# Adding up the squares of the inner norms on VectorE alone, taking their sums inside the third unit, and rotating the mixing projections over four banks

## The chip, the core and the metric

The program runs on one core of a Trainium2 chip. The core has a matrix engine (TensorE, PE in the profile), a vector engine (VectorE, DVE), an activation engine (ScalarE, ACT), a general engine (GpSimd, POOL) and a queue that issues DMA transfers (SP). The metric is the device time of one execution in microseconds (us); three executions of the kernel before took 1939.79 to 1940.9 us.

## The reference

Two transformer blocks work on the same 512 tokens of width 1024. Reduced to their order, they are:

```
h = h + 0.5 * swiglu(rmsnorm(h, ffn1_norm))            # norm "ffn1"
u = rmsnorm(h, mix_norm); projections u @ w_in          # norm "mix": three attentions, gates
h = h + sum(gates * branches) @ w_out
h = h + 0.5 * swiglu(rmsnorm(h, ffn2_norm))            # norm "ffn2"
z = rmsnorm_2(h, g_mix_2) @ w_in_2 + b_in_2             # norm "mix2": conv of 31 taps, pooling
h = h + y @ w_out_2
h = h + swiglu_2(rmsnorm_2(h, g_ffn_2))                 # norm "ffn3"
out = rmsnorm_2(h, g_final_2)                           # norm "final"
# rmsnorm(x, g) = x * rsqrt(mean(x*x) + eps) * g
```

## The kernel before, in words

Activations lie transposed: features on the 128 partitions, the 512 tokens along the row, so that a width of 1024 is eight chunks (`DK`). The weights are one stream of units of 128 x 1024 numbers; a unit projects the eight input chunks onto 128 outputs, or spreads one chunk over eight outputs. Every fp32 product is made of three matmuls on rounded numbers: high by high, weights low by high, high by input low (`products`, L458 to L460). One unit is 24 matmuls.

Four raw units and two split units fit in memory. For unit u, ScalarE writes the high part (`high`, L851), which needs unit u-2 to be done by TensorE (its slot in `weights_high` becomes free); GpSimd then writes the low part (`low_part`, L384), and TensorE waits for that (`low_done`) before its first matmul of u. `after(u)` on ScalarE stands for "cast unit u+2".

A norm's factor per token is not applied to the input but to the outputs of the projections. At such a norm the input is made chunk by chunk: VectorE updates the residual (L1199), ScalarE writes the high part of the chunk times the gain (L861) and its square (L862), VectorE the low part (L1163). Meanwhile TensorE runs `pair_start`: the first two units, interleaved, unit two three chunks behind unit one, each chunk as its low part comes. The squares of chunks 0 to 4 are added by GpSimd (L400, four additions), those of 5 to 7 and the total by VectorE (L1180, three additions). TensorE then sums over the partitions with narrow matmuls (`sums`, L511), ScalarE takes the root (L867), VectorE the inverse (L1170), TensorE spreads the result over the partitions (`spread_factor`, L519), and VectorE copies it out of the bank (`token_factor`, L1189). Only then can VectorE take the outputs of the first units (L1214 and on; L1247 in the mixing stage of the first block, L1508 in that of the second).

The order on every engine is the order in which the code is written; engines meet by semaphores. On ScalarE, in `gate_up`, the cast of a stage's fifth unit (`after(u0 + 2)`) stands behind the silu and the high part (L972) of the first hidden chunk, both of which need the factor. In the mixing stages (`stepped`, and the loop over `IN2_STEPS`), it stands behind the square, or the sigmoid, of the second projection. The mixing projections go round over three banks: unit j waits until the output of unit j-3 was taken. After a projection of the first mixing stage TensorE makes the head norms' sums (L583) and the transposes (L593) of the projection before. In the second mixing stage VectorE and GpSimd also add up the taps of a convolution (L1473 and L443), on inputs that ScalarE scales.

## Time and profile before

| | |
|---|---|
| median of three runs | 1940.22 us |
| the profiled execution, first to last instruction | 1940.7 us |
| TensorE busy | 1863.6 us (96%) |
| VectorE busy | 893.9 us (46%) |
| ScalarE busy | 660.9 us (34%) |
| GpSimd busy | 848.8 us (44%) |
| mean granted TensorE clock | 0.985 |

The profiled execution's span and the median of the unprofiled runs are half a microsecond apart. A row of the timeline gives the start, the duration, the engine, the line of the kernel and the operation with what it writes and reads; in brackets stands how long the engine had been idle before, and what ended that. Matmul rows overlap: what counts for TensorE is the distance between starts.

### The profile page before, as it was taken

The page shows a single profiled execution, that of the slowest core. Times are in us where ns is not written, and L with a number is a line of the kernel's source. Part 1 is how long each engine was busy: PE and PEld are TensorE (multiplying, and loading weights), DVE is VectorE, ACT ScalarE, POOL GpSimd, SP SyncE. Part 2 cuts the span into 40 slices and gives each one's busy share as a digit, 9 for nine tenths or more (in the row PEclk, how much of TensorE's full clock was granted, in tenths as well). Part 3 has the DMA queues.
Part 4 walks back from the last instruction along what each step waited for, and adds up shares of the span by engine and source line. Part 5 has one row for each costly group of instructions (what it writes and reads, how often), then busy time and mean ns, then how long its engine had stood idle before and what let it go on. Part 6 is the DMA issues. An engine that isn't in the chain of part 4 may idle for free.

```text
span 1940.7 us, 22811 instructions
## 1 busy us (share of the span) xinstructions
PE 1863.6 (96%) x8194; PEld 1456.3 (75%) x8194; DVE 893.9 (46%) x1254; ACT 660.9 (34%) x1003; POOL 848.8 (44%) x379
## 2 busy tenths in 40 slices
PE   7999999999999999999999999999967999999997
PEld 5888888778776566667878888888753778888886
DVE  4333330377776876446633333302799353333102
ACT  4332321353223444446333323211523343332212
POOL 4444444544444322323454444444664254444443
PEclk9999999999999999999999999999987999999998
DMA  4222222323332111111222222222210122222221
GB/s 170 97 97 97 97 98 94 118 81 104 112 99 83 60 55 39 36 42 55 101 84 98 97 97 97 97 95 95 87 55 33 58 84 97 97 97 97 98 97 54
DMA packets 48763, 167.38 MB, mean 86 GB/s; under 512 B 5816, under 2 KB 6328, under 8 KB 48576
## 3 DMA queue, kind: packets, MB, share of 16 engines
q1 hardware_dynamic: 45216, 160.27, 23.6%
q10 hardware_dynamic: 3488, 6.31, 1.0%
q8 instruction: 38, 0.62, 0.1%
q14 instruction: 21, 0.17, 0.0%
HBM read 161.82 MB, written 2.11 MB: 84 GB/s over the span
## 4 chain that ended last, share of the span: by engine, by line
PE 86%; DVE 10%; ACT 2%; issue 1%; DMA 1%; ACTq 0%; DVEq 0%; SPq 0%
PE bank L458 23%; PE bank L460 23%; PE bank L459 23%; PE bank L640 7%; PE bank L674 4%; DVE conv_out L1473 3%; PE bank L702 3%; DVE input_low L1163 1%; PE bank L687 1%; DVE head_root L1302 1%; PE bank L790 1%; DVE tile L1293 1%; PE bank L583 1%; DVE residual L1199 1%; DVE tile L1294 1%
## 5 line engine op out<-in xcount | busy, mean ns | idle before, releaser
L384 POOL TENSOR_TENSOR weights_low<-raw_weights,weights_high 128x1024 fp32r<-128x1024 f32 x296 | 732.1, 2473 | 1070.3 <-ACT weights_high L851 1070.1
L458 PE MATMUL bank<-input_high,weights_high 128*128 128x512 f32 x1488 | 594.3, 399 | 39.6 <-DVE input_low L1163 20.9
L851 ACT CAST weights_high<-raw_weights 128x1024 fp32r<-128x1024 f32 x296 | 311.2, 1051 | 923.7 <-PE bank L460 883.9
L459 PE MATMUL bank<-input_high,weights_low 128*128 128x512 f32 x1488 | 584.7, 393 | 0.0
L460 PE MATMUL bank<-input_low,weights_high 128*128 128x512 f32 x1488 | 584.3, 393 | 0.0
L458 PEld LDWEIGHTS bank<-input_high,weights_high 128*128 128x128 f32 x1488 | 282.7, 190 | 113.2 <-issue 32.5
L460 PEld LDWEIGHTS bank<-input_low,weights_high 128*128 128x128 f32 x1488 | 282.5, 190 | 60.4
L459 PEld LDWEIGHTS bank<-input_high,weights_low 128*128 128x128 f32 x1488 | 282.9, 190 | 59.7 <-issue 2.6
L458 PE MATMUL bank<-hidden_high,weights_high 128*128 (+1 forms) x528 | 205.4, 389 | 0.0
L459 PE MATMUL bank<-hidden_high,weights_low 128*128 (+1 forms) x528 | 205.4, 389 | 0.0
L460 PE MATMUL bank<-hidden_low,weights_high 128*128 (+1 forms) x528 | 205.4, 389 | 0.0
L1219 DVE TENSOR_TENSOR tile<-bank,token_factor 128x512 f32<-128x512 f32 x66 | 45.6, 691 | 305.2 <-PE bank L460 305.2
L1229 DVE TENSOR_TENSOR hidden_low<-tile,hidden_high 128x512 f32 x66 | 122.6, 1857 | 58.7 <-ACT hidden_high L972 58.7
L1199 DVE SCALAR_TENSOR_TENSOR residual<-bank,residual 128x512 f32<-128x512 f32 x40 | 27.1, 683 | 262.5 <-PE bank L460 262.5
L459 PEld LDWEIGHTS bank<-hidden_high,weights_low 128*128 128x128 f32 x528 | 99.1, 188 | 20.7
L458 PEld LDWEIGHTS bank<-hidden_high,weights_high 128*128 128x128 f32 x528 | 99.1, 188 | 20.5
L460 PEld LDWEIGHTS bank<-hidden_low,weights_high 128*128 128x128 f32 x528 | 99.1, 188 | 20.5
L640 PE MATMUL bank<-input_high,weights_high 128*128 128x512 f32 x192 | 83.2, 434 | 0.0
L1473 DVE SCALAR_TENSOR_TENSOR conv_out<-glu_padded,vectors,conv_out 128x512 f32<-128x512 f32 x67 | 80.5, 1202 | 2.1
L640 PE MATMUL bank<-input_low,weights_high 128*128 128x512 f32 x192 | 81.0, 422 | 0.0
L640 PE MATMUL bank<-input_high,weights_low 128*128 128x512 f32 x192 | 80.8, 421 | 0.0
L1214 DVE TENSOR_TENSOR tile<-bank,token_factor 128x512 f32<-128x512 f32 x66 | 45.6, 691 | 66.6 <-PE bank L460 65.7
(219 smaller groups left out, 1890.4 us busy)
## 6 DMA issues: line engine op xcount, KB each, us to landing
raw_weights<-weights SPq DMA_DIRECT2D x296, 512.0 KB, 3.3
tile<-tile ACTq DMA_DIRECT2D x36, 64.0 KB, 2.2
residual<-x_t SPq DMA_DIRECT2D x4, 512.0 KB, 8.5
tile<-forget_sums ACTq DMA_DIRECT2D x8, 256.0 KB, 3.2
out_t<-out_t SPq DMA_DIRECT2D x8, 256.0 KB, 2.1
mem_in<-mem_t ACTq DMA_DIRECT2D x1, 1024.0 KB, 6.0
causal_mask<-causal_mask SPq DMA_DIRECT2D x1, 256.0 KB, 7.7
positions_in<-positions SPq DMA_DIRECT2D x1, 256.0 KB, 9.4
```

The source lines that it names most:

```text
L384: pool.tensor_tensor(wl[:, u % SPL, :], raw[:, u % RAW, :], wh[:, u % SPL, :].bitcast(F32), ALU.subtract).then_inc(low_done, 1)
L458: pe.matmul(out, wh[:, u % SPL, w], rh, start=start, stop=False)
L459: pe.matmul(out, wl[:, u % SPL, w], rh, start=False, stop=False)
L460: return pe.matmul(out, wh[:, u % SPL, w], rl, start=False, stop=stop)
L640: mm = pe.matmul(bank[g % 2][:, :], (wl if part == 1 else wh)[:, u % SPL, w], (xl if part == 2 else xh)[:, k, :], start=(k == 0 and part = ...
L674: mm = pe.matmul(bank[3 + n % 2][:, 0:ext], left, right, start=True, stop=(kind != "fox"))
L702: mm = pe.matmul(heads_bank(chunk_id(n))[lo:hi, q * P:(q + 1) * P], val, probs_t[s % 2][:, b * P:(b + 1) * P], start=(b == 0), stop=(b == ...
L851: act.copy(wh[:, u % SPL, :], raw[:, u % RAW, :]).then_inc(high_done, 1)
L1199: dve.scalar_tensor_tensor(out=h[:, m, :], in0=bank[m][:, :], scalar=share, in1=h[:, m, :], op0=ALU.mult, op1=ALU.add).then_inc(sem("resid ...
L1214: dve.tensor_tensor(tiles[c][:, :], bank[2 * c][:, :], rstd[:, :], ALU.mult).then_inc(sem(f"{name}_gate"), 1)
L1229: dve.tensor_tensor(hl[:, f, :].rearrange("p a n -> p (a n)"), tiles[2 + c][:, :], hh[:, f, :].rearrange("p a n -> p (a n)").bitcast(F32), ...
L1473: ins = dve.scalar_tensor_tensor(out=conv[:, c, :], in0=src, scalar=w, in1=conv[:, c, :], op0=ALU.mult, op1=ALU.add)
```

## The change

GpSimd no longer adds squares at the norms ffn1, mix, ffn2, mix2 and ffn3; VectorE adds all seven behind its last low part. At the final norm the old division stays. `sums` moves from the end of `pair_start` into the middle of the third unit (between its chunks 3 and 4), and `spread_factor` from ahead of the third unit to behind it. On ScalarE the cast of the fourth unit moves ahead of the root. The mixing projections use four banks, so that unit j waits for the output of j-4. In the first mixing stage the sums and transposes of projections 0 and 1 move into the middle of the fourth unit.

```diff
-        proj = [bank[0], bank[1], bank[7]]
+        proj = [bank[0], bank[1], bank[7], bank[3]]
+        proj2 = [bank[0], bank[1], bank[7], bank[6]]
...
+        def totalled(name):
+
+            return (INPUTS.index(name) + 1) * (DK - 1) - (POOL_SQUARES - 1) * (name == "final")
...
             low_part(0)
             low_part(1)
-            add_squares("ffn1")
             low_parts(2, U_IN + 2)
-            add_squares("mix")
...
+            def project(u, out, rh, rl, low_at, n=S, halfway=None):
                 pe.wait_ge(low_done, low_at)
                 for k in range(DK):
+                    if halfway and k == DK // 2:
+                        halfway()
                     mm = products(out, u, k, rh[:, k, 0:n], rl[:, k, 0:n], k == 0, k == DK - 1)
...
-                pe.wait_ge(sem("squares_totalled"), (INPUTS.index(name) + 1) * (DK - POOL_SQUARES))
+                pe.wait_ge(sem("squares_totalled"), totalled(name))
...
                 pair_start(feed, u0, bank[0][:, :], bank[1][:, :])
+                project(u0 + 2, bank[2][:, :], xh, xl, u0 + 3, halfway=lambda: sums(feed))
                 spread_factor(feed)
-                project(u0 + 2, bank[2][:, :], xh, xl, u0 + 3)
                 project(u0 + 3, bank[3][:, :], xh, xl, u0 + 4)
...
+            def finish(i):
+
+                kind, n = IN_STEPS[i], tokens(IN_STEPS[i])
+                if kind in NORM:
+                    k = upto_step(IN_STEPS, NORM, i)
+
+                    pe.wait_ge(sem("in_squared"), k)
+                    if k > 1:
+                        pe.wait_ge(sem("in_rooted"), k - 1)
+                    pe.matmul(bank[2][:, 0:n], (bd if heads(kind) == 2 else ones)[:, :],
+                              sq_in[k % 2][:, 0:n], start=True, stop=True).then_inc(sem("in_summed"), 1)
...
-                        if j >= 3:
-
-                            pe.wait_ge(sem("in_taken"), j - 2)
+                        if j >= 4:
+
+                            pe.wait_ge(sem("in_taken"), j - 3)
                         if IN_STEPS[j] == "km" and chunk_of(IN_STEPS, j) == 0:
                             pe.wait_ge(sem("mem_low"), DK)
+                        rh, rl = (mem_h, mem_l) if n == MEM else (xh, xl)
+                        project(U_IN + j, proj[j % 4][:, 0:n], rh, rl, U_IN + j + 1, n,
+                                halfway={2: lambda: sums("mix"), 3: lambda: (finish(0), finish(1))}.get(j))
                         if j == 2:
                             spread_factor("mix")
...
+                    if 3 <= j <= n_steps:
+                        finish(j - 1)
...
-            pair_start("mix2", U_IN2, proj[0][:, :], proj[1][:, :])
+            pair_start("mix2", U_IN2, proj2[0][:, :], proj2[1][:, :])
             for j in range(2, len(IN2_STEPS)):
-                if j >= 3:
-
-                    pe.wait_ge(sem("in2_taken"), j - 2)
+                if j >= 4:
+
+                    pe.wait_ge(sem("in2_taken"), j - 3)
+                project(U_IN2 + j, proj2[j % 4][:, :], xh, xl, U_IN2 + j + 1,
+                        halfway=(lambda: sums("mix2")) if j == 2 else None)
                 if j == 2:
                     spread_factor("mix2")
...
-                        after(U_IN + j)
+                        if j != 1:
+                            after(U_IN + j)
                         if j == 0:
+                            after(U_IN + 1)
                             feed_root("mix", bank[4])
...
                         after(u0 + 2 * c, i)
                         if c == 0 and i is None:
+                            after(u0 + 1)
                             feed_root(feed_name, bank[4])
-                            after(u0 + 1)
...
-                after(U_IN2 + j)
+                if j != 1:
+                    after(U_IN2 + j)
                 if j == 0:
+                    after(U_IN2 + 1)
...
+                for m in range(1, DK):
+                    dve.wait_ge(sem("input_square"), fed(name, m))
+                    dve.tensor_tensor(tiles[0][:, :], tiles[0][:, :], tiles[m][:, :], ALU.add
+                                      ).then_inc(sem("squares_totalled"), 1)
+                    dve.wait_ge(sem("squares_totalled"), INPUTS.index(name) * (DK - 1) + m)
```

On TensorE, at the norm ahead of the second feed-forward network (ffn2), before: `L511` are the sums, `L519` the spread, and the row that waits for `low_done` opens the third unit.

```order
L460 MATMUL bank<-input_low,weights_high 128x512
L511 MATMUL bank<-ones,tile_102 128x1 [waits squares_totalled]
L511 MATMUL bank<-ones,tile_102 128x1 x3
L519 MATMUL bank<-identity,token_root 128x128 [waits norm_inverse]
L519 MATMUL bank<-identity,token_root 128x128 x3
L458 MATMUL bank<-input_high,weights_high 128x512 [waits low_done]
L459 MATMUL bank<-input_high,weights_low 128x512
```

Now, at the same place, the third unit follows the pair at once. Its middle (L507 are the sums) reads:

```order
L455 MATMUL bank<-input_low,weights_high 128x512
L507 MATMUL bank<-ones,tile_102 128x1 [waits squares_totalled]
L507 MATMUL bank<-ones,tile_102 128x1 x3
L453 MATMUL bank<-input_high,weights_high 128x512
L454 MATMUL bank<-input_high,weights_low 128x512
```

And this is the seam between the third and the fourth unit now, with the spread (L515):

```order
L455 MATMUL bank<-input_low,weights_high 128x512
L515 MATMUL bank<-identity,token_root 128x128 [waits norm_inverse]
L515 MATMUL bank<-identity,token_root 128x128 x3
L453 MATMUL bank<-input_high,weights_high 128x512 [waits low_done]
L454 MATMUL bank<-input_high,weights_low 128x512
```

The sums moved by 12 matmuls, the spread by 24. On ScalarE, at the same norm, before (the casts are of the third, fourth, fifth and sixth unit of the stage, in this order):

```order
L851 CAST weights_high<-raw_weights 128x1024 [waits unit_done,raw_loaded2]
L867 ACT_TABLE_LOAD
L867 ACTIVATE token_root<-bank,epsilons 128x4 [waits norm_sum]
L851 CAST weights_high<-raw_weights 128x1024 [waits unit_done,raw_loaded3]
L967 ACT_TABLE_LOAD
L967 ACTIVATE tile_102<-tile_102 128x512 [waits g2_gate]
L972 CAST hidden_high<-tile_104 128x512 [waits g2_act]
L851 CAST weights_high<-raw_weights 128x1024 [waits unit_done,raw_loaded0]
L967 ACTIVATE tile_103<-tile_103 128x512 [waits g2_gate]
L851 CAST weights_high<-raw_weights 128x1024 [waits unit_done,raw_loaded1]
```

Now (L969 is the silu, L974 the high part of the hidden chunk):

```order
L851 CAST weights_high<-raw_weights 128x1024 [waits unit_done,raw_loaded2]
L851 CAST weights_high<-raw_weights 128x1024 [waits unit_done,raw_loaded3]
L867 ACT_TABLE_LOAD
L867 ACTIVATE token_root<-bank,epsilons 128x4 [waits norm_sum]
L969 ACT_TABLE_LOAD
L969 ACTIVATE tile_102<-tile_102 128x512 [waits g2_gate]
L974 CAST hidden_high<-tile_104 128x512 [waits g2_act]
L851 CAST weights_high<-raw_weights 128x1024 [waits unit_done,raw_loaded0]
```

The cast of the fourth unit moved ahead of the root; that of the fifth stands where it stood, behind `hidden_high`.

## Rows read from the trace of the kernel before

**Rows 1.** Waits of TensorE: waiter, releaser, total us, times, longest.
```profile
PE bank L458 <- DVE input_low L1163: 20.9, 6, 9.9
PE bank L458 <- POOL weights_low L384: 16.4, 7, 5.4
...
PE bank L458 <- DVE tile L1508: 1.8, 2, 1.0
```

**Rows 2.** Timeline of TensorE at ffn3: start, us, operation, idle before.
```profile
1562.17 0.50 PE L458 MATMUL bank<-input_high,weights_high 128*128 128x512 f32 x1 [2.32 <-DVE input_low L1163]
...
1572.52 0.95 PE L511 MATMUL bank<-ones,tile 128*128 128x1 f32 x8
1574.10 1.16 PE L519 MATMUL bank<-identity,token_root 128*128 128x128 f32 x8 [0.63 <-DVE token_root L1170]
1575.02 0.49 PE L458 MATMUL bank<-input_high,weights_high 128*128 128x512 f32 x1
...
1586.04 0.39 PE L458 MATMUL bank<-input_high,weights_high 128*128 128x512 f32 x1
```

**Rows 3.** Timeline of VectorE at ffn3.
```profile
1556.83 0.73 DVE L1163 SCALAR_TENSOR_TENSOR input_low<-residual,vectors,input_high 128x512 fp32r<-128x512 f32 x1
...
1559.78 2.33 DVE L1163 SCALAR_TENSOR_TENSOR input_low<-residual,vectors,input_high 128x512 fp32r<-128x512 f32 x1 [0.35 <-ACT input_high L861]
...
1562.64 1.17 DVE L1163 SCALAR_TENSOR_TENSOR input_low<-residual,vectors,input_high 128x512 fp32r<-128x512 f32 x1
...
1566.03 2.87 DVE L1163 SCALAR_TENSOR_TENSOR input_low<-residual,vectors,input_high 128x512 fp32r<-128x512 f32 x2
1568.83 2.13 DVE L1180 TENSOR_TENSOR tile<-tile,tile 128x512 f32<-128x512 f32 x3
...
1575.30 0.69 DVE L1189 COPY token_factor<-bank 128x512 f32<-128x512 f32 x1 [1.25 <-PE bank L519]
```

**Rows 4.** Timeline of GpSimd at ffn3.
```profile
1559.20 2.37 POOL L384 TENSOR_TENSOR weights_low<-raw_weights,weights_high 128x1024 fp32r<-128x1024 f32 x1 [3.44 <-ACT weights_high L851]
1561.52 6.83 POOL L400 TENSOR_TENSOR tile<-tile,tile 128x512 f32<-128x512 f32 x4
1571.15 2.37 POOL L384 TENSOR_TENSOR weights_low<-raw_weights,weights_high 128x1024 fp32r<-128x1024 f32 x1 [2.80 <-ACT weights_high L851]
...
1581.99 2.40 POOL L384 TENSOR_TENSOR weights_low<-raw_weights,weights_high 128x1024 fp32r<-128x1024 f32 x1 [4.81 <-ACT weights_high L851]
```

**Rows 5.** Timeline of ScalarE at ffn3.
```profile
1570.02 1.06 ACT L851 CAST weights_high<-raw_weights 128x1024 fp32r<-128x1024 f32 x1 [2.63 <-PE bank L460]
...
1578.44 0.62 ACT L972 CAST hidden_high<-tile 128x512 fp32r<-128x512 f32 x1 [0.76 <-DVE tile L1224]
1580.86 1.05 ACT L851 CAST weights_high<-raw_weights 128x1024 fp32r<-128x1024 f32 x1 [1.80 <-PE bank L460]
```

**Rows 6.** Stretches from restart to pair's end (ffn2, ffn3): busy, PEclk, DMA, GB/s.
```profile
1007.00:1018.30 11.30, 10.65 (x41) 8.68 (x41) 9.36 (x11) 6.07 (x8) 7.96 (x6) 0.85 0.13 48
...
1562.10:1572.60 10.50, 10.28 (x41) 7.19 (x41) 8.79 (x11) 6.08 (x8) 7.47 (x5) 1.00 0.15 50
```

**Rows 7.** Timeline of VectorE in the second mixing stage (mix2).
```profile
1386.88 0.69 DVE L1189 COPY token_factor<-bank 128x512 f32<-128x512 f32 x1 [1.25 <-PE bank L519]
...
1400.81 1.21 DVE L1511 SCALAR_TENSOR_TENSOR glu_padded<-tile,vectors,glu_gate 128x512 f32<-128x512 f32 x1 [2.30 <-ACT glu_gate L1114]
...
1403.49 10.67 DVE L1473 SCALAR_TENSOR_TENSOR conv_out<-glu_padded,vectors,conv_out 128x512 f32<-128x512 f32 x5
1414.19 0.69 DVE L1508 TENSOR_TENSOR tile<-bank,token_factor 128x512 f32<-128x512 f32 x1
```

**Rows 8.** Timeline of VectorE in the first mixing stage (mix).
```profile
401.22 0.38 DVE L1264 TENSOR_TENSOR log_forget<-bank,vectors 128x8 f32<-128x8 f32 x4 [2.69 <-PE bank L593]
```

**Rows 9.** Timeline of ScalarE there.
```profile
410.73 0.69 ACT L910 ACTIVATE head_root<-bank,epsilons 128x512 f32<-128x512 f32 x1
```

**Rows 10.** Timeline of TensorE there.
```profile
413.91 1.02 PE L583 MATMUL bank<-tile,ones_by_head 128*128 128x512 f32 x2
```

More of the change, by code:

```diff
@@ L277, in added @@
             return fed(name, m) - DK
-        def squares(name):
-            return (INPUTS.index(name) + 1) * (POOL_SQUARES - 1) + (DK - 1) * (name not in ("ffn1", "mix"))
+        def totalled(name):
+            return (INPUTS.index(name) + 1) * (DK - 1) - (POOL_SQUARES - 1) * (name == "final")
         def nth(name):
@@ L432, in _ @@
             low_parts(U_BR + 2, U_GU2 + 2)
-            add_squares("ffn2")
             low_parts(U_GU2 + 2, U_IN2 + 2)
-            add_squares("mix2")
             tap = 0
@@ L447, in _ @@
             low_parts(U_WO2 + 2, U_GU3 + 2)
-            add_squares("ffn3")
             low_parts(U_GU3 + 2, UNITS)
-            add_squares("final")
+            add_last_squares()
         @block.tensor
@@ L501, in pair_start @@
                             mm.then_inc(unit_done, 1)
-                sums(name)
             def sums(name):
@@ L551, in down @@
                     spread_unit(name, u0 + f, hh[:, f, :], hl[:, f, :], u0 + f + 1, last=(f == FC - 1))
+            def finish(i):
[7 more added lines that the diff above has]
+                              sq_in[k % 2][:, 0:n], start=True, stop=True).then_inc(sem("in_summed"), 1)
+                if kind in TURN:
+                    k = upto_step(IN_STEPS, TURN, i)
+                    pe.wait_ge(sem("in_taken"), i + 1)
+                    if k > 2:
+                        pe.wait_ge(sem("in_turned_out"), k - 2)
+                    lo = HD if kind in ("ik", "dk") else 0
+                    for b in range(n // P):
+                        mm = pe.transpose(bank[4 + k % 2][:, b * P:b * P + P - lo],
+                                          t_in[i % 4][lo:P, b * P:(b + 1) * P], ident[lo:P, lo:P])
+                    mm.then_inc(sem("in_turned"), 1)
             def stepped(fill):
@@ L567, in stepped @@
                         if j == 2:
                             spread_factor("mix")
-                        rh, rl = (mem_h, mem_l) if n == MEM else (xh, xl)
-                        project(U_IN + j, proj[j % 3][:, 0:n], rh, rl, U_IN + j + 1, n)
                     else:
                         fill(FILLS[j - n_steps])
-                    for i in ((0, 1) if j == 2 else (j - 1,)):
-                        if i >= n_steps:
-                            continue
-                        kind, n = IN_STEPS[i], tokens(IN_STEPS[i])
-                        if kind in NORM:
-                            k = upto_step(IN_STEPS, NORM, i)
-                            pe.wait_ge(sem("in_squared"), k)
-                            if k > 1:
-                                pe.wait_ge(sem("in_rooted"), k - 1)
-                            pe.matmul(bank[2][:, 0:n], (bd if heads(kind) == 2 else ones)[:, :],
-                                      sq_in[k % 2][:, 0:n], start=True, stop=True).then_inc(sem("in_summed"), 1)
-                        if kind in TURN:
-                            k = upto_step(IN_STEPS, TURN, i)
-                            pe.wait_ge(sem("in_taken"), i + 1)
-                            if k > 2:
-                                pe.wait_ge(sem("in_turned_out"), k - 2)
-                            lo = HD if kind in ("ik", "dk") else 0
-                            for b in range(n // P):
-                                mm = pe.transpose(bank[4 + k % 2][:, b * P:b * P + P - lo],
-                                                  t_in[i % 4][lo:P, b * P:(b + 1) * P], ident[lo:P, lo:P])
-                            mm.then_inc(sem("in_turned"), 1)
@@ L606, in stepped @@
                     if j == MEM_STEP + 11:
-                        pe.wait_ge(sem("squares_added"), squares("mix") + DK - 1)
+                        pe.wait_ge(sem("squares_added"), DK - 1)
                         for b in range(MEM // P):
@@ L1172, in total_squares, with total_last_squares @@
             def total_squares(name):
+                for m in range(1, DK):
[3 more added lines that the diff above has]
+                    dve.wait_ge(sem("squares_totalled"), INPUTS.index(name) * (DK - 1) + m)
+            def total_last_squares():
+                first = INPUTS.index("final") * (DK - 1)
                 for i, m in enumerate((*range(POOL_SQUARES + 1, DK), 0)):
                     if m:
-                        dve.wait_ge(sem("input_square"), fed(name, m))
+                        dve.wait_ge(sem("input_square"), fed("final", m))
                     else:
-                        dve.wait_ge(sem("squares_added"), squares(name))
+                        dve.wait_ge(sem("squares_added"), DK - 1 + POOL_SQUARES - 1)
                     total = tiles[POOL_SQUARES] if m else tiles[0]
@@ L1181, in total_squares @@
                                       ).then_inc(sem("squares_totalled"), 1)
-                    dve.wait_ge(sem("squares_totalled"), INPUTS.index(name) * (DK - POOL_SQUARES) + i + 1)
+                    dve.wait_ge(sem("squares_totalled"), first + i + 1)
             def factor(name):
@@ L1573, in _ @@
             feed("final", None, "g3", UNITS - 1, 1.0, parts=False)
-            total_squares("final")
+            total_last_squares()
             inverse("final")
```

10 lines of the change are left out of this document (4 added, 6 removed).

## The prediction

> **What bounds the kernel.** I read the page's busy shares first: TensorE is busy 96% of the span, so any time that TensorE gains or idles at a norm is a gain or loss of the whole, except where VectorE leads. Then the waits of TensorE [rows 1]: 20.9 us for low parts of the input and 16.4 us for low parts of weights. The wait for a bank that the fourth bank could remove is 1.8 us in all. Last I read the timelines around ffn3, the norm ahead of the third feed-forward network, engine by engine [rows 2 to 5]; ffn1, ffn2 and mix have the same pattern. There TensorE restarts at 1562.17 on the low part of chunk 3 and ends the pair of units at 1572.52; sums, root, inverse and spread take until 1575.02, with 0.63 us idle; units three and four follow, and unit five starts at 1586.04.
>
> **What the change removes.** The distance of starts of back-to-back matmuls is 0.23 us (48 in 11.02 us, 1575.02 to 1586.04) [rows 2]. From the restart to the pair's end 39 are issued in 10.35 us, which back to back would be 9.1 with the slower first one. A low part alone takes 0.73 us, but 2.33 while GpSimd splits weights, and 1.17, or 2.87 for two, while GpSimd adds squares [rows 3, 4]. So without the four GpSimd additions the pair ends some 1.3 us earlier, at 1571.2. The low part of 2.33 us stays: it collides with the weights' low part, not with the additions. At ffn2 this gain is not there: the granted clock is 0.85 over 11.30 us, against 1.00 at ffn3 [rows 6], so that (1 - 0.85) x 11.30 = 1.7 us go to the half level (1.2 in place of 2.4 GHz), and TensorE itself is the slow one. The rows show the clock falling after one pause of 2.3 us and not after an equal one.
>
> The Trainium skill, "SBUF — State Buffer", section "Who interferes with whom", says that VectorE and GpSimd share a port pair, that a VectorE instruction with two SBUF inputs contends with a GpSimd instruction that reads SBUF, and that the one that comes first blocks the other wholly. The durations above agree (1559.20 + 2.37 = 1561.57, and the low part ends 0.54 later). This rule speaks for taking the additions off GpSimd, and against the seven additions in a row, which now meet GpSimd's low parts; if the two shared the bandwidth instead, ffn3 would come out 1.1 us cheaper and mix2 likewise.
>
> **What it adds, replayed at ffn3.** (1) The third unit now starts right behind the pair, and needs its weights' low part. Its cast stood 2.50 us ahead of the pair's end and its low part ended at 1571.15 + 2.37 = 1573.52, 1.0 after that end [rows 2, 4, 5]. Before, the sums and the root lay over this second; now TensorE waits for it, 1.0 to 1.1 us, more than the 0.63 idle that it saves. (2) VectorE's additions cost 0.71 each (2.13 for three) [rows 3]. The low parts end near 1566.7 now (1566.03 + 2.87 = 1568.90, less 2 x 0.44 and 2.87 - 1.46); seven additions would be done at 1571.7. But GpSimd's low part for unit three wants to start at 1569.9: it gets in behind the fifth addition at 1570.25 and holds the sixth until 1572.6, and the low part for unit four holds the seventh until 1575.6, done 1576.2. Unit three starts at 1572.65, its middle is at 1575.4: TensorE waits 0.8 us there. (3) Sums 0.95, second half 2.75: unit three ends at 1579.9; spread 0.92; 1580.8. (4) The factor's copy comes 1.20 behind the spread's start, 1581.1, against 1575.30, 5.8 later. (5) The high part of the first hidden chunk follows the copy by 1578.44 - 1575.30 = 3.14: 1584.25 [rows 3, 5]. Behind it, in ScalarE's order, stands the cast of unit five, which before started at 1580.86, released by TensorE. Now it starts at 1584.8, its low part 1.13 later (1581.99 - 1580.86) and takes 2.40 [rows 4]: 1588.35. TensorE is through with unit four at 1580.8 + 5.5 = 1586.3 and waits 2.1 us. Unit five starts at 1588.4 against 1586.04: **+2.4 us**. What is queued behind the late cast (the sixth unit's) has more than a unit's time, 5.5 us, and is not late.
>
> At ffn2, with the pair held by the clock, no addition is late (seven end before the low part for unit three starts), and no pair time is gained: 1.1 + 12 matmuls 2.75 + 0.95 + 2.75 to the spread, and from its start 1.20 + 3.14 + 0.55 + 1.13 + 2.40, is 16.0 us from the pair's end to unit five, against 13.5 (1586.04 - 1572.52) before: **+2.5**. ffn1 is the same chain, with additions that end in time; its pair gains between 0 and 1.3 us, I take 0.2, as loading sets its pace: **+2.3**.
>
> **mix.** The factor is 6 us late (16.0 less 7.2 for the last steps gives 8.8 behind the pair, before 2.8). VectorE waited 2.69 us for the transposes there [rows 8], and these are now later too. The root of the third projection ended at 411.42, and TensorE's head sum of the fourth came at 413.91 [rows 9, 10]: a slack of 2.5 us, hence between 0 and 3.5 us of loss; VectorE's idle time eats some two of the six, and I take **+1.4**. The four banks gain nothing: no wait for `in_taken` is in rows 1 here.
>
> **mix2.** Here VectorE leads: it goes without a pause from 1403.49 to 1414.19 and on, and TensorE waits for it [rows 1, 7]. Five taps take 10.67 us, against 3.7 at 0.73 each, because GpSimd works beside them. So the whole delay of the factor counts: +5.8 as at ffn3. Bounds: VectorE's pause of 2.30 us ahead of 1400.81 goes, since the projection is long there, which gives 3.5 at the low end. But GpSimd's work that lay under this pause and under reads of banks now meets taps: one weights' low part, 2.4, and two tap additions of 1.1 (6.83 / 4 less the 0.6 of VectorE's turn) make 4.6. If no pause went, that would be 5.8 + 4.6 = 10.4, the high end. I take both: 5.8 - 2.3 + 4.6 = **+8.1**. The bank waits of 1.8 us lie in this stage, behind them TensorE waits for weights that ScalarE casts after VectorE's outputs: the fourth bank gains nothing.
>
> **The clock.** TensorE gets new pauses of 2.1 us at ffn1, ffn2 and ffn3, near those of 2.3 us of which some are followed by the half clock. None to three more such stretches at 1.7 us; I take one: **+1.7**. The final norm is unchanged: 0.
>
> **Sum.** 2.3 + 1.4 + 2.5 + 8.1 + 2.4 + 1.7 = 18.4 us. On the profiled 1940.7 that is 1959.1; the median of the runs lies 0.5 below the profiled span: 1958.6, say 1959.
>
> **Rivals.**
> A. Smaller loss: the stages absorb. VectorE in mix2 finishes only 3.5 us late, mix loses nothing, the clock nothing, and the additions slip in between low parts (ffn3 1.3). 2.3 + 0 + 2.5 + 3.5 + 1.3 = 9.6: 1950. For it: the pause of 2.30 us [rows 7]. Against: TensorE's 1.0 and 2.1 us waits don't hang on it.
> B. Faster. The point from which it decides is whether unit five's low part is ready when unit four ends: the hidden chunk's high part would have to come 2.1 us sooner, and VectorE in mix2 to be held by nothing. Then TensorE alone counts: at five norms a wait of 1.1 us in place of 0.63 idle, -2.3; pairs quicker by 1.3 at mix2, ffn3 and ffn1, +3.9; and with all low parts on time the half clock at mix and ffn2 gone, +3.4: 5.0 us, 1935. For it: the idle 0.63 and the slowed low parts are real [rows 2, 3]. Against: the order of the casts, and that the pause of 2.3 us ahead of the clock's fall stays.
> C. The half clock follows each of the three new pauses and two more in mix2: 4 x 1.7 more, 1966.
> D. The moves cancel: the pairs' gain at mix2 and ffn3, 2.6, and the wait of 1.1 for 0.63 at five norms, 2.3: 1940. That, too, needs unit five and VectorE in mix2 on time.
>
> **Chances.** Forecast (1953 to 1963) 0.55; A 0.20; C 0.11; B 0.08; D 0.06. The range 1947 to 1967 leaves out B and D and a little of A and C. The measurement can tell about 0.2% (3.9 us) from no change. Slower by more: the forecast, A and C, 0.86; within: D, 0.06; faster: B, 0.08.
>
> **What would show it.** In the profile after: TensorE's first matmul of the third unit idle about 1 us for GpSimd's low part at five norms (step 1); `sums` idle for VectorE at the norms whose pair runs at the full clock (2); the cast of unit five directly behind `hidden_high`, and TensorE idle some 2 us for it at three norms (5); in mix2 the copy of the factor 5 to 6 us later relative to the restart and VectorE's third pair of projections 8 us later (mix2). No low part of 1.17 us any more. The forecast is wrong if unit five starts on time, or if VectorE in mix2 catches up before the taps end.

## The result and the profile after

The changed kernel takes 1959.48 us (median of 4, 1959.13 to 1960.47), the kernel before in the same comparison 1940.56 (1939.79 to 1942.27): a ratio of 1.0099, 95% interval 1.0085 to 1.0113, slower. 1959.0 was predicted, with 1947 to 1967.

The page of the changed kernel, first its part 1, then the shares of the chain of part 4:

```profile
span 1957.3 us, 22810 instructions
...
PE 1863.0 (95%) x8194; PEld 1455.4 (74%) x8194; DVE 914.2 (47%) x1274; ACT 660.4 (34%) x1003; POOL 818.6 (42%) x359
...
PE 77%; DVE 11%; issue 7%; POOL 2%; ACT 2%; DMA 1%; ACTq 0%; DVEq 0%; SPq 0%; POOLq 0%
```

TensorE's busy time is that of before, 1863 us: all that was lost is idle time of TensorE. GpSimd is 30 us less busy, VectorE 20 more. TensorE's waits in the changed kernel (waiter, releaser, total us, times, longest):

```profile
PE bank L453 <- POOL weights_low L384: 32.4, 17, 6.5
PE bank L453 <- DVE input_low L1167: 20.2, 6, 9.1
...
PE bank L453 <- DVE tile L1325: 2.7, 1, 2.7
...
PE bank L558 <- ACT head_root L912: 1.1, 1, 1.1
PE bank L507 <- DVE tile L1180: 1.0, 3, 0.3
```

Against [rows 1] the wait for weights' low parts has doubled, from 16.4 us in 7 places to 32.4 in 17; three kinds of wait are new (L1325, `head_root`, and `sums` at L507), the wait for a bank has gone, and so have the five of 0.63 us for the inverse ahead of the spread. L1325 is the VectorE copy that prepares the second forget matmul of the first mixing stage (`forget_out`).

The loss by stages, each from one restart of TensorE on the low part of chunk 3 (as in [rows 2]) to the next, in us:

| stretch | before | after | difference | predicted |
|---|---|---|---|---|
| start to first restart | 14.55 | 13.74 | -0.8 | 0 |
| ffn1 | 367.26 | 367.79 | +0.5 | +2.3 |
| mix and the attention behind it | 625.84 | 630.10 | +4.3 | +1.4 |
| ffn2 | 366.12 | 370.45 | +4.3 | +2.5, and 1.7 for the clock |
| mix2 | 188.40 | 194.68 | +6.3 | +8.1 |
| ffn3, to the last norm's sums | 365.82 | 367.89 | +2.1 | +2.4 |

With the unchanged tail that is 16.6 us, the difference of the profiled spans. The medians differ by 18.9, since the profiled execution of before was itself about 2 us above its median: the difference of time and span is 1.8 us in the execution after (1959.13 and 1957.3), and by the same 1.8 that of before took some 1942.5.

**At ffn3.** TensorE in the changed kernel (start, us, operation, idle before):

```profile
1587.16 0.50 PE L453 MATMUL bank<-input_high,weights_high 128*128 128x512 f32 x1 [1.25 <-POOL weights_low L384]
1590.51 1.05 PE L507 MATMUL bank<-ones,tile 128*128 128x1 f32 x8 [0.34 <-DVE tile L1180]
1602.56 0.50 PE L453 MATMUL bank<-input_high,weights_high 128*128 128x512 f32 x1 [1.78 <-POOL weights_low L384]
```

The stage restarts at 1576.76, and the pair ends at 1587.16 - 1.25 = 1585.91, 9.15 us later, where it took 10.35 [rows 2]. Then come the three waits of the forecast: for the third unit's low part (L453, 1.25 us), for the seventh addition at the sums (L507, 0.34 us), for unit five's low part (L453, 1.78 us). ScalarE's rows show why unit five waits:

```profile
1598.48 0.62 ACT L974 CAST hidden_high<-tile 128x512 fp32r<-128x512 f32 x1 [0.76 <-DVE tile L1237]
1599.01 1.05 ACT L851 CAST weights_high<-raw_weights 128x1024 fp32r<-128x1024 f32 x1
```

The cast (L851) has no idle time ahead of it: it stands directly behind the hidden chunk's high part, where before it waited 1.80 us for TensorE [rows 5].

**In mix2**, VectorE of the changed kernel:

```profile
1386.61 9.18 DVE L1180 TENSOR_TENSOR tile<-tile,tile 128x512 f32<-128x512 f32 x7
...
1400.68 0.69 DVE L1202 COPY token_factor<-bank 128x512 f32<-128x512 f32 x1 [3.21 <-PE bank L515]
...
1404.87 10.66 DVE L1486 SCALAR_TENSOR_TENSOR conv_out<-glu_padded,vectors,conv_out 128x512 f32<-128x512 f32 x5
...
1417.64 0.75 DVE L1524 SCALAR_TENSOR_TENSOR glu_padded<-tile,vectors,glu_gate 128x512 f32<-128x512 f32 x1 [0.79 <-ACT glu_gate L1118]
...
1429.63 0.69 DVE L1521 TENSOR_TENSOR tile<-bank,token_factor 128x512 f32<-128x512 f32 x1
```

The factor is copied 18.60 us behind the restart at 1382.08, against 1386.88 - 1373.77 = 13.11 [rows 7]: 5.5 us later. VectorE's second pause for a sigmoid (ahead of 1417.64) is 0.79 us, where it was 2.30 [rows 7]. The first five taps take 10.66 us. In the kernel before, the same five took 5.92:

```profile
1391.06 5.92 DVE L1473 SCALAR_TENSOR_TENSOR conv_out<-glu_padded,vectors,conv_out 128x512 f32<-128x512 f32 x5
```

### The profile page after: what moved, and what is told of

It reads as the page before. It is cut to its first block, busy times and chain, and to the rows that moved or that the text cites. A ratio compares the mean times of both kernels' runs of the same rounds, so it can differ in the third digit from the quotient of the medians.

```text
span 1957.3 us, 22810 instructions
## 1 busy us (share of the span) xinstructions
PE 1863.0 (95%) x8194; PEld 1455.4 (74%) x8194; DVE 914.2 (47%) x1274; ACT 660.4 (34%) x1003; POOL 818.6 (42%) x359
## 4 chain that ended last, share of the span: by engine, by line
PE 77%; DVE 11%; issue 7%; POOL 2%; ACT 2%; DMA 1%; ACTq 0%; DVEq 0%; SPq 0%; POOLq 0%
PE bank L453 20%; PE bank L455 20%; PE bank L454 20%; PE bank L639 7%; PE bank L673 4%; DVE conv_out L1486 3%; PE bank L701 3%; POOL weights_low L384 2%; DVE head_root L1315 1%; PE bank L686 1%; DVE tile L1180 1%; DVE tile L1306 1%; DVE input_low L1167 1%; DVE tile L1307 1%; DMA tile<-tile 1%
## 5 line engine op out<-in xcount | busy, mean ns | idle before, releaser
L453 PE MATMUL bank<-input_high,weights_high 128*128 128x512 f32 x1488 | 593.8, 399 | 55.3 <-POOL weights_low L384 32.4
L851 ACT CAST weights_high<-raw_weights 128x1024 fp32r<-128x1024 f32 x296 | 311.1, 1051 | 899.2 <-PE bank L455 859.6
L453 PEld LDWEIGHTS bank<-input_high,weights_high 128*128 128x128 f32 x1488 | 282.9, 190 | 128.4 <-issue 37.3
L453 PE MATMUL bank<-hidden_high,weights_high 128*128 (+1 forms) x528 | 205.4, 389 | 0.0
L453 PEld LDWEIGHTS bank<-hidden_high,weights_high 128*128 128x128 f32 x528 | 99.1, 188 | 20.4
```

Source lines behind the costliest of these rows:

```text
L453: pe.matmul(out, wh[:, u % SPL, w], rh, start=start, stop=False)
L851: act.copy(wh[:, u % SPL, :], raw[:, u % RAW, :]).then_inc(high_done, 1)
```

## The experiments

Each kernel was compared with the kernel before on the same chip. That kernel took 1940.6 to 1941.0 us in the first two groups and 1942.3 in the last (`combo`, `combo_mix`). The theory: TensorE loses by the order of its waits, the placing of the sums costs in every stage, and the cast order in the feed-forward stages is a cost by itself. The rivals: VectorE's longer chain of additions is the cost, or the waits only change their names.

**sq_only: the additions alone.** From the kernel before; sums, spread and casts stay, three banks.

```
-            add_squares("ffn1")          # GpSimd, likewise mix, ffn2, mix2, ffn3
...
+                for m in range(1, DK):   # VectorE, all seven
+                    dve.wait_ge(sem("input_square"), fed(name, m))
+                    dve.tensor_tensor(tiles[0][:, :], tiles[0][:, :], tiles[m][:, :], ALU.add
+                                      ).then_inc(sem("squares_totalled"), 1)
...
```

> The kernel before with one part alone: at the five inner norms VectorE adds all seven squares and GpSimd none; sums, spread, casts and the three banks stand as before. Theory A (the loss of the whole change comes from where sums, spread and the factor stand): this part costs little, since at ffn1 the pair is quicker by 2.0 us (its pair took 9.7 us from the restart after, 11.7 before), and at norms whose pair runs at the full clock the seventh addition ends 2.3 us behind the pair's end (restart + 11.4 against + 9.1), 1 us later than the sums stood before: 1938 to 1943 us. Theory B (VectorE's longer chain of additions is the loss): 1950 us or more. What the profile should show under A: sums idle for VectorE 1.5 to 2.5 us at two or three norms, low parts of 0.75 us in place of 1.17.

Measured: 1950.8 us (4 runs, 1949.93 to 1951.79), ratio 1.0055 (1.0038 to 1.0072). The expectation of 1938 to 1943 us missed, and the rival's 1950 us or more is what came. TensorE at mix and at ffn2, then the clock over the pair at mix (busy by engine, PEclk, DMA share, GB/s):

```profile
392.31 1.62 PE L505 MATMUL bank<-ones,tile 128*128 128x1 f32 x8 [2.50 <-DVE tile L1170]
...
1023.37 1.25 PE L505 MATMUL bank<-ones,tile 128*128 128x1 f32 x8 [2.53 <-DVE tile L1170]
```

```profile
380.60:389.80 9.20, 9.17 (x39) 7.24 (x39) 8.90 (x13) 6.08 (x8) 1.49 (x1) 1.00 0.17 59
```

Where the pair runs at 2.4 GHz it is 1.2 us shorter, and the seventh addition then ends 2.5 us behind it. The half clock follows this wait: the granted clock is 0.67 over the 10.20 us behind the pair at mix and 0.70 over 11.20 us at ffn2, some 3.4 us each. The trace puts the loss there: mix is 3.7 us longer up to the attention, ffn2 4.0, and no other feed-forward or mixing stage is more than 0.3 us longer. In mix2 and at ffn3 this execution had the pair itself at the half clock (0.84), and nobody waited there. So VectorE's chain of additions does cost, at the old place of the sums, and most of its price is the clock. At the new place the wait is down to 0.34 us.

**place_only: the placing alone.** The changed kernel with GpSimd's four additions and three banks, so sums, spread, casts and the transposes stand where the change puts them. These moves were made together; the order of the fourth unit's cast and the place of the transposes were not tested by themselves.

```
+            add_squares("ffn1")          # GpSimd again, likewise the other four
...
-        proj = [bank[0], bank[1], bank[7], bank[3]]
+        proj = [bank[0], bank[1], bank[7]]
...
```

> The changed kernel with the squares divided as before (GpSimd four, VectorE three) and three banks: only sums, spread, casts and head sums stand in their new places. Theory A: all of the loss is here, and the pairs' gain of 1.3 to 2 us per norm is missing, while the wait of 0.3 us for the seventh addition goes: 1959 to 1965 us, with TensorE idle 1.1 us ahead of the third unit at five norms and 1.8 us ahead of unit five at three. Theory B: near before, 1940 to 1945 us.

Measured: 1967.19 (1966.2 to 1968.48), ratio 1.0140 (1.0123 to 1.0157), 2.2 us above the expected range. This part costs 26.6 us, more than the whole change, and the rival's 1940 to 1945 us is far off: both parts cost when they stand alone. Its waits, of which the first is the wait for a bank:

```profile
PE bank L458 <- DVE tile L1517: 9.1, 4, 3.0
...
PE bank L563 <- ACT head_root L917: 2.7, 3, 1.1
PE bank L458 <- DVE tile L1321: 2.7, 1, 2.7
```

**banks_only: the four banks alone**, on the kernel before.

```
-        proj = [bank[0], bank[1], bank[7]]
+        proj = [bank[0], bank[1], bank[7], bank[3]]
+        proj2 = [bank[0], bank[1], bank[7], bank[6]]
```

> The kernel before with the fourth bank for both mixing stages and nothing else. My theory: nothing, 1940.5 plus or minus 1 us; the waits of 0.84 and 0.99 us for an output taken by VectorE vanish and come back as waits for the weights' low part behind them. Rival (the bank wait is on the path): 1938.7 us.

Measured: 1940.92 (10 runs, 1939.63 to 1948.48), ratio 1.0006 (0.9992 to 1.0021): no difference. The bank waits of [rows 1] are gone, and the waits for weights behind them are longer:

```profile
PE bank L459 <- POOL weights_low L385: 17.4, 7, 6.6
```

**cast5: unit five's cast ahead of the first silu**, on the changed kernel.

```
-                        after(u0 + 2 * c, i)
+                        if c == 0 or i is not None:
+                            after(u0 + 2 * c, i)
...
+                        if c == 0 and i is None:
+                            after(u0 + 2)
                         act.wait_ge(sem(f"{name}_gate"), one)
```

> The changed kernel, with ScalarE's cast of unit five in the three feed-forward stages ahead of the first silu (it is ready once TensorE has done unit three, before the factor is there). My theory: the three pauses of 1.76 us ahead of unit five go, 5.3 us, and with them a stretch at the half clock of 1.7 us if it followed one of them: 1952.5 to 1954.5 us. Rival (the late factor holds the stage in another place too, such as VectorE's outputs or unit six): the pause moves to a later unit, 1958 to 1960 us.

Measured: 1958.15 (1951.83 to 1960.16), ratio 1.0083 (1.0062 to 1.0104). The median stands in the rival's range, 4 us above the expected one, and one run of four is at 1951.83, so the times alone don't decide it. The trace does: the three waits for unit five are gone, ffn2 is 3.7 us shorter (370.45 to 366.79), ffn3 2.1 (367.89 to 365.82). At ffn2 of the changed kernel a stretch of half clock stood behind the wait of 1.76 us (0.78 over 7.7 us, 1.7 us). No wait of its length stands at a later unit, so the rival falls. What hides the gain in this execution is a stretch of half clock at the start of the attention, where the kernel pauses 2.16 us in every version: from this pause to TensorE's next wait of over 1 us, in the attention over the memory, it takes 295.8 us, against 291.2 in the changed kernel. The clock there, in the changed kernel and in this one:

```profile
600.00:640.00 40.00, 37.84 (x133) 21.84 (x132) 25.39 (x42) 12.74 (x24) 16.03 (x9) 1.00 0.24 79
```

```profile
600.00:640.00 40.00, 37.84 (x117) 21.60 (x115) 21.38 (x33) 11.76 (x22) 15.92 (x9) 0.87 0.22 68
```

**forget_late: the wait for `forget_out` at the forget matmul**, on the changed kernel.

```
-                    if j == 6:
-                        pe.wait_ge(sem("forget_out"), 1)
                     if j == MEM_STEP + 11:
+                        pe.wait_ge(sem("forget_out"), 1)
```

> The changed kernel, with TensorE's wait for the blend's forget product moved from the seventh chunk of the second mixing projection to the chunk just before the forget matmul. The theory (the forget product now ends behind a late factor, and TensorE meets it too early): the wait of 2.70 us on the VectorE tile of L1325 goes and the mix ends 2 to 2.7 us earlier, about 1956.8 us. The rival (the wait only moves to another product of VectorE further on, such as the one that frees a bank of the projection): a wait of 2 to 3 us stands elsewhere in the mix and the time stays at about 1959.5 us.

Measured: 1957.55 (1957.06 to 1965.35), ratio 1.0086 (1.0071 to 1.0100), about 2 us below the changed kernel; 1956.8 was expected. Its profiled execution is the 1965.35, with 17 us at the half clock at the start of the attention; the mixing stage can be read all the same. Up to the attention it takes 216.77 us, not 221.32: 4.5 less, 2.70 of them the wait. The rest is the clock, in the changed kernel (first row) and without the wait:

```profile
433.00:441.10 8.10, 7.24 (x25) 5.78 (x26) 6.20 (x7) 1.91 (x4) 1.88 (x2) 0.79 0.21 65
```

```profile
437.00:445.00 8.00, 8.00 (x35) 6.24 (x34) 7.38 (x8) 2.85 (x6) 4.94 (x4) 1.00 0.21 66
```

0.21 x 8.1 = 1.7 us. No wait took its place, so the rival falls.

**mix2_old: the old place of sums and spread in mix2 alone**, VectorE's additions and the four banks kept.

```
+                    sums("mix2")
+                    spread_factor("mix2")
+                project(U_IN2 + j, proj2[j % 4][:, :], xh, xl, U_IN2 + j + 1)
```

> The changed kernel, but at the second mixing stage alone the sums and the spread of the factor stand where they stood before: at the end of the pair of units, with the fourth unit's cast behind the root on ScalarE. VectorE still adds all the squares and the four banks stay. The theory (there the late factor delays the whole chain of VectorE's mixing products, and TensorE waits for the low parts of the second mix at the end): the stretch from the restart of the second mixing stage to the restart of the third feed-forward stage falls from 194.7 us to 189 to 191, with a new wait of 0.3 to 2.5 us for the seventh addition at the sums and the third unit's wait of 1.28 us gone; about 1954.5 us. The rival (the slower stretch is due to the projections' four banks or to VectorE's longer chain of additions, not to the place of the sums): the stretch stays at 193 or more and the time at 1958 to 1960 us.

Measured: 1957.43 (1952.01 to 1960.1), ratio 1.0084 (1.0069 to 1.0098). The stretch of mix2 is 188.52 us against 194.68 after and 188.40 before: the placing of the sums, the spread and the fourth unit's cast is the whole loss of this stage, and in this execution neither the additions nor the banks cost anything there. VectorE shows it:

```profile
1389.62 5.04 DVE L1178 TENSOR_TENSOR tile<-tile,tile 128x512 f32<-128x512 f32 x7
...
1398.20 0.69 DVE L1200 COPY token_factor<-bank 128x512 f32<-128x512 f32 x1 [1.25 <-PE bank L515]
...
1402.38 5.92 DVE L1484 SCALAR_TENSOR_TENSOR conv_out<-glu_padded,vectors,conv_out 128x512 f32<-128x512 f32 x5
```

The restart is at 1385.09 and the copy 13.11 behind it, as before; the seven additions take 5.04 us, since no weights' low part cuts in, and the first five taps 5.92, as in the kernel before, where they took 10.66 after. The pair ran at the half clock here (0.87 over 10.6 us), so the wait of up to 2.5 us for the seventh addition didn't come. The median fell by 2 us only, to 3 us above the expected 1954.5; the runs spread over 8 us.

**three_banks: the changed kernel with three banks.** The edit is that of `banks_only` backwards.

> The changed kernel with the mixing projections on three banks again. The theory (once the factor is late, VectorE empties the banks late, and the fourth bank takes TensorE's waits for them away): waits for a bank of 1.5 to 3 us each come back at one to two places of the mix and three to four of the second mixing stage, of which the later waits of TensorE for the low parts take back most; about 1961 us, up to 1965. The rival (the fourth bank only renames waits, as in the kernel before): bank waits show, the waits for low parts at the end of the second mixing stage are shorter by as much, and the time is within 1 us of 1959.5 us.

Measured: 1965.75 (1964.66 to 1966.94), ratio 1.0131 (1.0116 to 1.0145): 6.3 us slower than with four, above the range of both theories. The bank waits are back:

```profile
PE bank L452 <- DVE tile L1520: 8.3, 4, 3.0
```

with one of 1.51 us in the mix more. That stage up to the attention takes 225.6 us, and mix2 195.7. The changed kernel's 221.3 and 194.7 are no fair measure for them, since its pairs ran at 2.4 GHz there and those of this execution did not (0.85 over the pair in both stages). `cast5` has four banks, the same code in these stages and its pairs at the same low clock (0.84 and 0.86): 221.9 and 195.5. So of the 6.3 us the traces locate 3.7 in the mix, where besides the bank wait two waits for `head_root` (0.76 and 0.90 us) are new, and 0.2 in mix2, where the bank waits stand in for waits for weights. The rest is not located. The fourth bank is worth nothing with the factor at its old time, and with the late one it is worth about 4 us by the traces and 6 by the times.

This kernel and `place_only` differ only in who adds the squares: 1.0131 against 1.0140. VectorE's chain, which costs 10 us at the old place of the sums, costs nothing that the times show at the new one.

**half_spread: only the spread into the third unit's middle**, in the three feed-forward stages of the kernel before.

```
-                spread_factor(feed)
-                project(u0 + 2, bank[2][:, :], xh, xl, u0 + 3)
+                project(u0 + 2, bank[2][:, :], xh, xl, u0 + 3, halfway=lambda: spread_factor(feed))
```

> The kernel before, with one edit: in the three feed-forward stages the spread of the factor over the partitions stands in the middle of the third unit and the sums stay at the end of the pair. The theory: TensorE no longer waits about 0.63 us between the sums and the spread in each stage, the third unit starts at once with its weights ready, and the factor is late by less than the third unit's own work: 1938.7 us (0.6 us in each of three stages). The rival (the third unit then waits for the weights' low part, as where the sums were moved as well, or a later unit for its activation): 1940 to 1943 us.

Measured: 1939.94 (12 runs, 1938.54 to 1947.46), ratio 0.9998 (0.9985 to 1.0011). Three of the five waits of 0.63 us for the inverse are gone, two of 0.23 and 0.20 us for the third unit's low part are new at ffn1 and ffn2, and ffn2 and ffn3 are 0.4 and 0.5 us shorter in the trace. So small a gain can't be told from none in the times.

**combo: cast5, forget_late and mix2_old together.**

> The changed kernel with the three repairs together: unit five's cast ahead of the first silu, the wait for the blend's forget product at the forget matmul, and the old place of the sums at the second mixing stage. VectorE still adds all squares; the sums of the other four inner norms stay in the third unit. The theory (the three costs are separate): waits of 1.76 us for unit five, 2.70 us for L1325 and the longer second mixing stage are all gone, 7.8, 2.7 and 6.2 us less than 1959.5 us: 1943 us, range 1941 to 1947, so what is left over the kernel before is four waits of about 1.2 us for the third unit's low part. The rival (the repairs take back the same time, as TensorE's later waits absorb what an earlier one gives): 1950 us or more, with new or longer waits at the end of the second mixing stage.

Measured: 1947.55 (10 runs, 1944.57 to 1955.06), ratio 1.0034 (1.0019 to 1.0048). Its ten times lie in two heaps, 1944.6 to 1949.4 (7) and 1953.7 to 1955.1 (3), the latter at a lower mean clock (0.979 against 0.983 to 0.984). The median is 0.6 us above the expected range and 2.4 below the rival's. The profiled execution (1945.17) has a span of 1943.4, 13.9 us under 1957.3; 16.7 was expected, and by the medians it is 12 us. So the three costs are separate for the most part, not in full. What is left over the kernel before stands mostly in the mix: 217.7 us up to the attention, against 215.5. Its third unit waits 1.11 us, and 1.08 and 0.15 us of waits for `head_root` follow:

```profile
382.53 0.50 PE L453 MATMUL bank<-input_high,weights_high 128*128 128x512 f32 x1 [2.33 <-DVE input_low L1167]
...
394.40 0.50 PE L453 MATMUL bank<-input_high,weights_high 128*128 128x512 f32 x1 [1.11 <-POOL weights_low L384]
...
415.51 1.10 PE L558 MATMUL bank<-tile,ones_by_head 128*128 128x512 f32 x2 [0.15 <-ACT head_root L911]
...
425.60 1.10 PE L558 MATMUL bank<-tile,ones_by_head 128*128 128x512 f32 x2 [1.08 <-ACT head_root L911]
```

**combo_mix: combo, and the old place in the first mixing stage too.**

> As the kernel with the three repairs, and at the first mixing stage too the sums and the spread stand at the pair's end as before. The theory (at a pair that runs at full clock VectorE's seven additions are late by 2.5 us at the pair's end, so there the third unit is the better place once its followers are repaired): the wait for the sums is 2.5 us at 392 us, the third unit's wait of 1.25 us is gone, the stage is 1 to 4 us longer by the half clock that follows, and the time is 1 to 3 us above that kernel. The rival (the late factor costs more than the wait): the mixing stage is 1 to 3 us shorter, and the time is below it by as much.

Measured: 1951.16 (6 runs, 1943.16 to 1952.64), ratio 1.0039 (1.0026 to 1.0052). It can't be told from `combo`: the intervals overlap. The wait of 2.5 us at the sums didn't come in the profiled execution, for its pair ran at the half clock (0.84 over 10.65 us), and the stretch is 217.3 against 217.7 us: the expected numbers missed, and which place is better at mix stays open.

No kernel tried is faster than the kernel before.

## Why the prediction was right, and where it was right by luck

**The third unit's wait (1)** was put at 1.0 to 1.1 us; it is 0.96, 1.25, 1.11, 1.28 and 1.25 at the five norms. Right.

**The additions (2).** A pair quicker by 1.3 us, with no gain at the half clock; measured 10.35 to 9.15 at ffn3, and at ffn2, from the restart to the pair's end, 10.57 before and 10.74 after. The additions take 9.18 us in mix2, with two low parts between them, and 7.19 at ffn1, where one comes. The wait of 0.8 for the seventh is 0.34 at ffn3, 0.33 in mix2, and 0.34 at mix, whose pair ran at the full clock this time. The term was put at more than double its size. A term of that size hid what `sq_only` showed: at the pair's end the seventh addition is 2.5 us late, and only the new place of the sums makes it harmless.

**The factor (4) and unit five (5).** 5.8 us later was 5.5; the wait of 2.1 us for unit five was 1.76, 1.76 and 1.78, from the order on ScalarE as told, and `cast5` removes it. Right.

**ffn1** is the term most off: +2.3 forecast, +0.5 found. The waits are there (0.96 and 1.76, for 0.63 saved). In this execution TensorE came to the full clock before its restart (the first matmul takes 0.50 us, those behind it 0.39), in the profiled one of before 3 us behind it (0.80 us, its successors 0.63 until 17.7 us). Its pair took 9.8 us. In five kernels with the same code there that met the slower start (`cast5`, `forget_late`, `mix2_old`, `three_banks`, `combo`) it took 11.4 to 11.9. Three of them have the same code in all of ffn1: `three_banks` took 369.7 us, 2.4 over the kernel before, and `forget_late` and `mix2_old` 371.5, with a stretch of half clock behind the wait for unit five (0.79 over 8.0 us, 0.78 over 7.6). So the code's own cost is near the forecast, and the low number came from the clock of this execution.

**mix** failed by a missing step: +1.4 forecast, +4.3 found. The forecast asked of head sums and transposes, and found 1.4 us. It did not look at `pe.wait_ge(sem("forget_out"), 1)` at j == 6, which had slack before. VectorE gets to L1325 51.7 us behind the restart (433.19 - 381.53), where it was 46.9 (428.67 - 381.81 for the same copy), and TensorE stands 2.70 us, with 1.7 of half clock behind. `forget_late` removes both, and what remains is 216.77 - 215.46 = 1.3 us, by the number the 1.4 of the forecast. The profiled execution of before had its pair at the half clock here (10.79 us). `banks_only`, with the same order and its pair at the full clock (10.36), took 215.05, so with equal clocks 1.7 us remain, still near the forecast. But they are made otherwise: the pair is 1.2 us quicker, and against that stand the third unit's wait of 1.25 us for 0.63 saved, 0.34 at the sums, 1.09 for `head_root`, and short gaps. Later 1.6 us came back, because a stretch at the half clock at the start of the attention in before wasn't there after.

**ffn2 and the clock.** 2.5 + 1.7 forecast, 4.3 found, and the stretch of half clock does stand behind unit five's wait. The other such stretch stood in the mix, behind the wait that was not foreseen. So "one of three" was two of four. Which wait is followed by the half clock changes with the execution: behind the same wait for unit five at ffn2 it did not come in `forget_late`, `mix2_old` and `three_banks` (368.9 us for the stage, not 370.5), and in the first two it came at ffn1. That the one forecast stretch came was right in size and luck in place.

**mix2**: +8.1 forecast, +6.3 found. The bounds were 3.5 and 10.4. At its third pair of projections VectorE is 1429.63 - 1382.08 = 47.55 us behind the restart, against 1414.19 - 1373.77 = 40.42 [rows 7]: 7.1 late, where 8.1 were forecast. The rows split these 7.1. The copy is 5.5 late (5.8). The first five taps take 4.7 us more (10.66 for 5.92), and GpSimd is busy for 9.95 us beside them, where it was for 3.41: this is its work that now meets the taps, put at 4.6. The pause shrank by 1.5 us (2.30 to 0.79), not by 2.3. The term that was left out is the work that GpSimd no longer slows: the two instructions behind the pause, 1.21 and 1.40 us before (the first is in [rows 7]), take 0.75 and 0.55 now, 1.3 us less, with GpSimd busy for 0.29 us beside them, not 2.57. TensorE's stage is then only 6.3 us longer. The place of the loss is shown by `mix2_old`.

**ffn3**: +2.4 forecast, +2.1 found. 1.25 + 0.34 + 1.78 of waits less 0.63 and less 1.2 for the pair is 1.5. Of the rest some 0.5 is in the 48 matmuls of units three and four, which without sums, spread and waits take 11.55 us, against 11.02 [rows 2]: behind each interruption the next matmul starts 0.31 to 0.34 us later, not 0.23.

**The four banks** "gain nothing" is right on the kernel before (`banks_only`) and wrong on this one: without them it is 6 us slower (`three_banks`). The forecast looked for bank waits in the trace of before, where the factor was early. It had itself made the factor 6 us late, and should have asked the question again after that.

**The sum** was 18.4 us on the profiled execution, and 16.6 were found there. Stage by stage the errors are -1.8 at ffn1, +2.9 in mix, +0.1 at ffn2, -1.8 in mix2, -0.3 at ffn3, and -0.8 ahead of the first restart: the wait that was overlooked in mix is made good by terms put too high and by the clock of one execution. The second step was the 0.5 taken off for the median. It set a time against a span, while an execution takes 1.8 us more than its span, and it took the profiled execution of before for a usual one, while that was 2 us slow: from the pause at the start of its attention to the attention over the memory it took 292.7 us, where `half_spread`, with the same code there, took 291.2. After the change the median lies 2.2 us above the profiled span, not 0.5 below. So the sum was 1.8 us too high and the step to the median more than 2 too low, and a hit by 0.5 us was luck. Right by reasoning were the direction, the third unit's wait, the late factor with unit five behind it, and the delay in mix2; the range of 20 us was the honest statement.

## What to carry to other kernels

Moving a small reduction into the shade of the next work saves a pause of 0.6 us and makes its result late by several; count what hangs on the result on every engine, in program order, and most of all the semaphore waits that had slack. Parts of a change don't add up: 10 us for the additions alone and 27 for the placing alone gave 19 together, since the placing hides the additions (`three_banks` is no slower than `place_only`) and the fourth bank hides part of the placing. After a step has shifted a time, ask again of every wait that was nothing before.

## What the runs showed of the hardware

The clock makes a short wait dear, but not each time. In the changed kernel waits of TensorE of 1.76 us (unit five at ffn2) and 2.70 us (mix) were followed by a stretch at the lower level that cost 1.7 us, while the equal waits for unit five at ffn1 and ffn3 (1.76 and 1.78 us) were not; in `forget_late` the one at ffn1 was and those at ffn2 and ffn3 were not. In `sq_only` two waits of 2.5 us were followed by stretches that cost 3.4 us each. The pause of 2.16 us at the start of the attention is the same in all versions. In seven profiled executions the granted clock stayed at 1.00 over the next 25 us, and from the pause to the attention over the memory it took 291.2 us. In the other five it was 0.93 (before), 0.86 (`sq_only`), 0.80 (`cast5`), 0.73 (`banks_only`) and 0.66 (`forget_late`), and the same work took 292.7, 294.3, 295.8, 297.3 and 298.9 us. That by itself moves an execution by up to 8 us, and it is the likely reason, not shown for the runs without a trace, why three of ten runs of `banks_only` took 1945.57 to 1948.48 with a median of 1940.92. A profiled execution should be held against the list of times before its segments are compared.

Seven chained additions of 128x512 on VectorE take 5.04 us with GpSimd idle (`mix2_old`) and 9.18 with two weights' low parts on GpSimd (5.53 us for both) in between (the changed kernel in mix2). The sum of both would be 10.6, so the two engines nearly take turns.
